# A diffusion trunk layer on one Trainium2 core: stores left under way at a stage's end, a routing search with bf16 counts, and a first gather by groups

## The reference, cut to what matters

```
def ec_moe(h, p):
    xt = h.reshape(T, D)
    aff = jax.nn.softmax((xt @ p["w_router"]).astype(F32), axis=-1)
    cap = (EC_CAPACITY_FACTOR * T) // N_EXPERTS
    vals, idx = lax.top_k(aff.T, cap)
    xs = xt[idx]
    hid = jax.nn.silu(einsum(xs, w_e_gate)) * einsum(xs, w_e_up)
    ye = einsum(hid, w_e_down) * vals[..., None]
    y = jnp.zeros((T, D)).at[idx.reshape(-1)].add(ye.reshape(-1, D))
```

## Time and profile before

| what | us |
|---|---|
| median of 3 runs | 3444.71 |
| the runs | 3438.53, 3444.91, 3444.71 |
| the profiled execution, its own time | 3445.33 |
| its span | 3443.2 |
| PE busy in it | 3199.8 (93%) |
| DVE busy | 1607.1 (47%) |
| ACT busy | 1271.0 (37%) |
| POOL busy | 363.5 (11%) |
| mean granted clock of TensorE | 0.957 |

### The profile page before, as it was taken

One profiled execution on the slowest core, in us unless ns is written; L12 is line 12 of the kernel. 1 busy time (PEld: TensorE's weight loads), 2 busy tenths in 40 slices (PEclk: granted clock), 3 DMA queues, 4 the chain that ended last, 5 costly groups with the idle time before them and its releaser, 6 DMA issues. The chain is left out here.

```text
span 3443.2 us, 51395 instructions
## 1 busy us (share of the span) xinstructions
PE 3199.8 (93%) x19321; PEld 2723.1 (79%) x19321; DVE 1607.1 (47%) x2990; ACT 1271.0 (37%) x1957; POOL 363.5 (11%) x313
## 2 busy tenths in 40 slices
PE   7899998999898799999989964999999999999996
PEld 2488886988644699989977753898888898899895
DVE  5423222533256442333235556555555555555555
ACT  4743342422243131222124531444444443344445
POOL 1111111000034100000000001111111111111122
PEclk9899999999899799999999985999999999999998
DMA  8633333321299751432125442555555555555557
GB/s 333 239 126 104 104 121 107 116 70 63 78 365 348 246 161 57 133 96 99 57 89 180 155 161 91 170 201 188 186 186 180 179 173 173 174 192 198 192 205 275
DMA packets 282677, 565.67 MB, mean 164 GB/s; under 512 B 23464, under 2 KB 162472, under 8 KB 278329
## 3 DMA queue, kind: packets, MB, share of 16 engines
q1 hardware_dynamic: 258063, 503.84, 41.9%
q0 software_dynamic: 15456, 54.88, 5.4%
q10 hardware_dynamic: 8976, 4.46, 0.5%
HBM read 434.45 MB, written 128.64 MB: 164 GB/s over the span
## 5 line engine op out<-in xcount | busy, mean ns | idle before, releaser
L71 PE MATMUL experts_bank<-experts_xT_high,experts_w_high_gu 128*128 128x272 f32 x2048 | 599.0, 292 | 6.2 <-DVE experts_w_low_gu L2998 6.2
L73 PE MATMUL experts_bank<-experts_xT_high,experts_w_low_gu 128*128 128x272 f32 x2048 | 591.4, 289 | 0.0
L72 PE MATMUL experts_bank<-experts_xT_low,experts_w_high_gu 128*128 128x272 f32 x2048 | 590.3, 288 | 0.0
L71 PEld LDWEIGHTS experts_bank<-experts_xT_high,experts_w_high_gu 128*128 128x128 f32 x2048 | 386.5, 189 | 19.1 <-issue 12.2
L72 PEld LDWEIGHTS experts_bank<-experts_xT_low,experts_w_high_gu 128*128 128x128 f32 x2048 | 386.9, 189 | 4.0
L73 PEld LDWEIGHTS experts_bank<-experts_xT_high,experts_w_low_gu 128*128 128x128 f32 x2048 | 386.9, 189 | 0.0
L2998 DVE TENSOR_TENSOR experts_w_low_gu<-experts_w_raw_gu,experts_w_high_gu 128x1024 fp32r<-128x1024 f32 x256 | 302.4, 1216 | 13.2 <-ACT experts_w_high_gu L2797 13.2
L2797 ACT ACTIVATE experts_w_high_gu<-experts_w_raw_gu 128x1024 fp32r<-128x1024 f32 x256 | 257.7, 1047 | 17.0 <-DMA experts_w_raw_gu<-in_w_stream 17.0
L71 PE MATMUL merge_pg<-merge_hT_high,merge_w_gates_high 128*128 128x436 f32 (+1 forms) x640 | 232.7, 364 | 12.5 <-DVE merge_hT_low L2093 12.5
L72 PE MATMUL merge_pg<-merge_hT_low,merge_w_gates_high 128*128 128x436 f32 (+1 forms) x640 | 231.9, 362 | 0.0
L73 PE MATMUL merge_pg<-merge_hT_high,merge_w_gates_low 128*128 128x436 f32 (+1 forms) x640 | 231.5, 362 | 0.0
(11 more groups left out here) (387 smaller groups left out, 6590.0 us busy)
## 6 DMA issues: line engine op xcount, KB each, us to landing
experts_w_raw_gu<-in_w_stream SPq DMA_DIRECT2D x256, 512.0 KB, 5.8
experts_w_raw_d<-in_w_stream SPq DMA_DIRECT2D x128, 512.0 KB, 7.5
filters_wm<-in_w_mod SPq DMA_DIRECT2D x12, 2048.0 KB, 11.6
merge_hT<-scratch_hT SPq DMA_DIRECT2D x32, 436.0 KB, 7.0
scratch_h<-out_row SPq DMA_DIRECT2D x17, 520.0 KB, 2.9
x_early<-in_xs SPq DMA_DIRECT2D x17, 512.0 KB, 5.2
scratch_hT<-tokens_hT SPq DMA_DIRECT2D x17, 512.0 KB, 4.2
scratch_qkT<-tokens_qkT SPq DMA_DIRECT2D x17, 512.0 KB, 2.8
```

The costliest lines, as they stand in the source:

```text
L71: pe.matmul(out, lhs[0], rhs[0], start=start, stop=False)
L72: pe.matmul(out, lhs[0], rhs[1], start=False, stop=False)
L73: return pe.matmul(out, lhs[1], rhs[0], start=False, stop=stop)
```

## The change

In the output stage SP no longer waits for its last stores: the four waits are kept in a list and done by SP at the head of the expert stage, which then gives POOL a semaphore (`stored`) that POOL waits for before the first gather. `x` and `row` are placed first in the stage's memory, where in the next stage only raw weights lie. `band` and `seg` are loaded in the output stage, and ACT makes a bf16 copy of `seg` at its end.

In the search, the context comparison goes from DVE to POOL (three tensor_scalar of 128x16, output bf16), the reduce is gone, and PE sums the 16 columns with 16 accumulating bf16 matmuls. The counts are bf16 (whole numbers up to 256). The context comparison with the capacity comes first, the latent one second.

The first gather has a semaphore for each group. PE turns group by group (8 blocks of one group, then the next), ACT and DVE treat a group in one instruction each; the second `index` no longer stands behind DVE's last low part.

```diff
 phase_out
+                sp.dma_start(s["band"][:], d["band"]).then_inc(s["ld_band"], 16)
+                sp.dma_start(seg[:], d["seg"]).then_inc(lds, 16)
                 stores(0, 0, 0, True)
...
                 retire(sp, s)
                 for h in range(2):
-                    sp.wait_ge(xst[h], 16 * ((NT + 1 - h) // 2) + HAD)
-                    sp.wait_ge(rst[h], 16 * ((NT + 1 - h) // 2) + HAD)
+                    s["open"].append((xst[h], 16 * ((NT + 1 - h) // 2) + HAD))
+                    s["open"].append((rst[h], 16 * ((NT + 1 - h) // 2) + HAD))
...
                 router(NT - 1, 0)
+                act.wait_ge(lds, 16)
+                act.activation(s["seg"][:], seg[:], ACT.Copy)
 phase_experts, SP
-                sp.dma_start(band[:], d["band"]).then_inc(ldb, 16)
-                sp.dma_start(seg, d["seg"]).then_inc(lds, 16)
+                for each, value in s["open"]:
+                    sp.wait_ge(each, value)
+                sp.sem_inc(stored, 1)
 PE
                 for i in range(DIGITS):
+                    pe.wait_ge(PB.sem, PB.at(i, "reach"))
+                    for t in range(CCAP):
+                        mm = pe.matmul(pn, seg_b[:, 0:P], reach[:, :, t], start=(t == 0), stop=(t == CCAP - 1))
+                    mm.then_inc(*QC.inc("sum"))
                     pe.wait_ge(RB.sem, RB.at(i, "count"))
-                    pe.matmul(pi[:, 0:6], seg[:, 0:P], cnt[:], start=True, stop=True).then_inc(*QB.inc("sum"))
+                    pe.matmul(pi[:, 0:3], seg_b[:, 0:P], cnt[:], start=True, stop=True).then_inc(*QB.inc("sum"))
...
                 index(0)
-                pe.wait_ge(ga, 48)
-                for q in range(KT):
-                    turn(q, bank[:, q, :])
-                pe.wait_ge(VX.sem, VX.at(0, f"x{KT - 1}"))
+                for n, (at, m) in enumerate(GROUPS):
+                    pe.wait_ge(g0[n], 16)
+                    for q in range(KT):
+                        mm = pe.transpose(first(n)[:, q, :], xs[0:m, n, P * q:P * q + P], s["ident"][0:m, 0:m])
+                    mm.then_inc(*P0.inc(f"g{n}"))
                 index(1)
 ACT
-                for q in range(KT):
-                    turned(0, 0, q, bank[:, q, :])
+                for n, (at, m) in enumerate(GROUPS):
+                    act.wait_ge(P0.sem, P0.at(0, f"g{n}"))
+                    act.activation(xh[:, 0, :, at:at + m], first(n), ACT.Copy).then_inc(*A0.inc(f"g{n}"))
 DVE
-                for steps in (VG, VM, VI, VX, VK, VD, VW, VF):
+                for steps in (VG, VM, VI, VX, VK, VD, VW, VF, V0):
                     steps.give(v)
+                v.sem_inc(VX.sem, KT)
...
-                    v.tensor_tensor(reach, few[:]..., cand[:, 1, :]..., ALU.is_ge).then_inc(*RB.inc("few"))
...
-                    v.wait_ge(RB.sem, RB.at(i, "few"))
-                    v.tensor_reduce(cnt[:, 3:6], reach, mybir.AxisListType.X, ALU.add).then_inc(*RB.inc("count"))
...
+                    v.wait_ge(QC.sem, QC.at(i, "sum"))
+                    v.tensor_scalar(met[:, 1, :], pn, float(CCAP), 0.0, ALU.is_ge, ALU.add,
+                                    accum_out=digit[:, 1:2]).then_inc(*RB.inc("mc"))
                     v.wait_ge(QB.sem, QB.at(i, "sum"))
...
+                for n, (at, m) in enumerate(GROUPS):
+                    v.wait_ge(A0.sem, A0.at(0, f"g{n}"))
+                    v.tensor_tensor(xl[:, 0, :, at:at + m], first(n), xh[:, 0, :, at:at + m].bitcast(F32), ALU.subtract)\
+                     .then_inc(*V0.inc(f"g{n}"))
 POOL
+                for i in range(DIGITS):
+                    if i:
+                        g.wait_ge(RB.sem, RB.at(i - 1, "cand"))
+                    else:
+                        g.wait_ge(R0.sem, R0.at(0, "bit"))
+                    for j in range(3):
+                        mm = g.tensor_scalar(reach[:, j, :], few[:], cand[:, 1, j:j + 1].bitcast(F32), None, ALU.is_ge)
+                    mm.then_inc(*PB.inc("reach"))
...
+                g.wait_ge(stored, 1)
                 gather(0, 0)
```

More of the change, by code:

```diff
@@ L2578, in phase_experts @@
         R0 = counted("dve_arrange", ["zero", "a0", "a1", "ac", "as", "prob", "few", "thr", "bit"])
-        RB = counted("dve_bits", ["few", "count", "bit", "next", "ml", "mc", "step", "cand", "thr"])
+        RB = counted("dve_bits", ["count", "bit", "next", "mc", "ml", "step", "cand", "thr"])
+        PB = counted("pool_bits", ["reach"])
         R1 = counted("dve_slots", ["gl", "gc", "need", "tl", "tc", "s0", "s1", "e0", "e1", "lim", "k0", "k1",
                                           "sel", "p0", "p1", "f0", "f1", "off", "q0", "q1", "pos", "ones"])
-        QB = counted("pe_bits", ["sum"])
+        QB, QC = counted("pe_bits", ["sum"]), counted("pe_bits_context", ["sum"])
         Q1 = counted("pe_route", ["prob", "above", "ahead", "slots", "pos"])
@@ L2586, in phase_experts @@
         PX = counted("pe_xT", [f"x{k}" for k in range(KT)])
+        P0, A0, V0 = (counted(f"{n}_xT_first", [f"g{n}" for n in range(len(GROUPS))]) for n in ("pe", "act", "dve"))
         PD = counted("pe_dn", [f"d{n}" for n in range(4)])
@@ L2986, in numbers @@
                     v.wait_ge(PI.sem, PI.at(e, "ids"))
[L2987 to L2988 removed]
+                    if e == 2:
+                        for sem in g0:
+                            v.wait_ge(sem, 16)
+                    elif e > 2:
+                        v.wait_ge(ga, e * 48 - 96)
                     v.tensor_copy(ids[:, h, 0:2], pi[:, 0:2]).then_inc(*VI.inc("i0"))
```

86 lines of the change are left out of this document (52 added, 34 removed).

## The result

The changed kernel takes **3420.01 us** (median of 4 runs, 3417.76 to 3422.66), the kernel before 3444.64 us (4 runs, 3438.53 to 3444.91): a ratio of 0.9934, 95% interval [0.9922, 0.9947].

What follows compares the result with a forecast made beforehand. A serial chain between the output stage and the gapless columns was taken as the bound; -1.0 - 1.1 + 0.2 - 9.8 - 1.3 - 4.8 = -17.8 us against 3445.33 gave 3427.5, for a median 3427, range 3421 to 3437.

Steps and rivals of the forecast that it cites:

- End of the output stage, -1.0: At the output stage's end nobody waits for the last row store any more: -1.0 us.
- two increments, +0.2: At the expert stage's start DVE has two more semaphore increments, 0.11 us each: +0.2 us.
- The band, -1.1: At the expert stage's start DVE's 1.08 us wait for the band goes, as it is loaded earlier: -1.1 us.
- The search, -9.8: In the search's 15 digits, a digit falls from 2.89 to 2.24 us, 0.65 us each: -9.8 us.
- margin of 0.1 us for POOL: In each digit POOL's three comparisons end at about 1.0 us, where about 1.1 is needed; the least certain term.
- Rival 2: In the search DVE's counts hold POOL, 0.47 us a digit slower than before: 3444, no change; chance 0.09.
- Rivals 1 and 3: Search: POOL's comparisons cost 0.4 us each, 3433, chance 0.15; each digit pays a 3.04 us hold, 3469, chance 0.05.
- The three sums, -1.3: Behind the search, three sums go from fp32 to bf16, 0.42 us less each: -1.3 us.
- The first gather, -4.8: Ahead of the columns, turning by groups hides the first group and starts columns at about 2125.9 instead of 2130.74: -4.8 us.
- PE's first turning: Sign in the profile at the first gather: PE starts turning some 6 us ahead of the last landing.

Runs made afterwards that it cites:

- e1: The kernel before, run again without an edit: 3443.78 us, ratio 1.0.
- e2: The changed kernel, run again without an edit: 3420.22 us, ratio to the kernel before 0.9934.
- e5: The kernel before with only the output stage's end changed (stores left under way, tables loaded ahead, memory laid out anew): 3439.08 us, ratio 0.9984.
- e11: The change without the first gather by groups: 3422.98 us, ratio to the kernel before 0.9935.
- e3: The kernel before with only the first gather by groups: 3439.0 us, ratio 0.9989.
- e4: The kernel before with only the new search and its bf16 sums: 3436.36 us, ratio 0.9976.
- e6: The kernel before with the new search and the gather by groups, without the output stage's changed end: 3430.87 us, ratio 0.9963.
- e10: The kernel before with DVE's comparisons for the second index held until POOL's three gather issues are out: 3437.85 us, ratio 0.9984.
- e12: The kernel before with new search and groups, plus one already met wait on POOL just ahead of the first gather: 3426.38 us, ratio 0.9949.
- e8: The change with one more POOL comparison in every digit: 3426.16 us, ratio to the kernel before 0.9951.
- e7: The change with POOL's wait for the stores moved to the start of its expert stage program: 3426.63 us, ratio to the kernel before 0.9945.
- e9: The change with DVE's comparisons for the second index held until POOL's three gather issues are out: 3424.77 us, ratio to before 0.9945.

## Why the prediction was right, and where it was off

**Right by its own steps.** The bound was read rightly: a serial chain in front of columns that then run on without a gap. From the first column to the first of the last expert's scattered adds it is 1206.0 us in e1 and 1204.6 in e2 (1204.6 to 1210.4 over the twelve), so what was gained ahead of the columns arrived at the end.

**End of the output stage, -1.0, and two increments, +0.2.** Both confirmed, the first a little larger. Router maximum to memset is 5.16 to 5.88 us in the seven profiles without the exit (mean 5.48) and 3.87 to 4.07 in the seven with it (mean 4.01): -1.5 us with what the increments cost. These belong to the groups: with the exit it is 3.87 and 3.88 us in e5 and e11, which have no groups, and 4.06 or 4.07 in the five profiles with them, so two increments cost 0.19 us, and the exit by itself is worth 1.6.

**The band, -1.1.** It is not there. Memset to band product is 2.44 us in the one profile that the forecast read, and 1.26 or 1.27 us in those of e1, e3, e4, e6, e10 and e12, which load the band as it does. The wait of 1.08 us was a late load in that execution, and a term was made of it.

**The search, -9.8.** The mechanism is right and the size slightly off: 2.33 us a digit and not 2.24. The step that failed is the margin of 0.1 us for POOL. Its start comes 0.26 us after `cand`, but the three comparisons are 0.29 us apart where 0.24 each was taken from a 128x1 row, and POOL ends at 1.16 us where 1.0 was expected and 1.1 was the latest that would do; DVE reads the context sum at 1.85 us instead of 1.75. Two of the 14 steps take 2.6 us. Over 15 digits the gain was 0.6 + 7.4 = 8.0 us.

**Rival 2, and the rule behind it, did not come.** POOL's comparisons and DVE's counts run at once with neither stretched: 0.40 us from count to count, as in the earlier trace rows. By the rule of the Trainium skill (Advanced Engine Details and Errata, VectorE Performance Modes) two-port instructions of VectorE and GpSimd's block each other; this trace shows no block for the counting form. Rivals 1 and 3 fell with the same rows.

**The three sums, -1.3.** Fifteenth `cand` to ids went from 15.82 to 14.62 us: -1.2.

**The first gather, -4.8: this is the step that was mis-sized.** It was priced with issues and landings carried over from the earlier trace rows. For the groups by themselves that held: 4.3 us (e3), 4.5 (e11 to e2). But 3.85 and 2.80 us were not the price of the issues. They were DVE's hold on them, and in the change the hold is gone: 23.7 us became 12.3 (e1 to e2), 11.4 in place of 4.8. PE's first turning came 2.8 us ahead of the last landing and not some 6. The forecast had seen a hold of 3.04 us on a small POOL operation and used it for a rival in the search, and did not ask whether the two long issues, with DVE busy beside them, were the same thing. The trace could have raised the question: of the 48 issues of this line in the kernel before the median takes 1.07 us, and the two of 128 rows here 3.85 and 2.80.

**The sum.** From e1 and e2, whose earlier stages agree within 0.12 us: exit with the increments -1.4, search -8.0, sums -1.2, gather -11.4, columns -1.4: -23.4 us. Their profiled executions differ by 3440.91 - 3417.24 = 23.7. Against these the forecast's -17.8 has 0.5 too much for exit, band and increments, 1.8 too much for the search, 0.1 too much for the sums, and 6.6 and 1.4 too little for gather and columns. The 1.4 of the columns is no larger than what they vary from profile to profile. That the total came as near as it did is in part luck: 2.4 us too much and 8.0 too little partly cancel.

**What decides whether the issues are held.** Shown: DVE's work holds them (e10, and the ends that keep their place). Why it does not in the change is open. With the first DMA 0.70 us after the ids, all six profiles beside a working DVE had long issues. With it at 1.19, behind the added wait, four had short ones (the change twice, e8, e11) and two long ones (e5, e12). That the wait must stand just ahead of the gather rests on e7. What the two long ones lack may be conditions as well: e5 the search (the groups are not one, by e11), e12 the exit's tables, its memory layout and the semaphore that is waited for. But each of these rests on one profile of one execution, and the times of e5 and e12 leave room for other executions in which the issues were short. So a hold that comes in some executions of one program and not in others is a rival that no run here settles; more profiles of e5, e7 and e12 would. In the change DVE pays a little instead: its 16 comparisons, 4.27 us in e12, are stretched to 4.75.

```profile
2092.20 4.75 DVE L3008 TENSOR_SCALAR experts_below<-experts_pos_slot 128x256 bf16<-128x256 f32 x16
```

```profile
2096.36 4.27 DVE L3004 TENSOR_SCALAR experts_below<-experts_pos_slot 128x256 bf16<-128x256 f32 x16
```

The first row is of the change, the second of e12. Most of the 0.48 us lies in three of the 16, where the others took 0.33 to 0.36 us each:

```profile
2094.03 0.48 DVE L3008 TENSOR_SCALAR experts_below<-experts_pos_slot 128x256 bf16<-128x256 f32 x1
...
2095.23 0.57 DVE L3008 TENSOR_SCALAR experts_below<-experts_pos_slot 128x256 bf16<-128x256 f32 x1
...
2096.50 0.44 DVE L3008 TENSOR_SCALAR experts_below<-experts_pos_slot 128x256 bf16<-128x256 f32 x1
```

The three issues of the change end at 2094.41, 2095.69 and 2096.84 us, each inside one of these. So near its end an issue and a comparison are in each other's way: here DVE gives way for 0.1 to 0.24 us, in e12 the issue waits 3.1 us. e11 and e12 start the DMA at the same moment against DVE's comparisons (1.19 us after the ids), and one is through in 1.17 us, the other in 4.28. What settles who gives way is not in the profile, and no run isolates it.

The Trainium skill (DMA: Bandwidth & Descriptors, SWDGE vs HWDGE vs iDMA) says that GpSimd writes the descriptors of its DMAs into SBUF, and that VectorE in a two-port mode locks it out of there. e10 agrees as to who holds whom; that the same comparisons let the issues through in the change, the page does not explain.

No version beat the change. It is the fastest run here, but 6.8 to 8.1 us of its path (e5 to e11, e7 to e2) hang on something that is not understood.

## What to carry to other kernels

Before a DMA issue's duration is carried into a sum, look at what VectorE does beside it, and compare it with the shortest issue of the same kind: here 3.85 us was a cost of 1.16. Where GpSimd's DMAs are on the path, try to let VectorE rest until they are issued: one wait gave the kernel before 7.2 us of path and 5.0 us of time. Where the issues go through anyway it costs instead: 2.0 us of path in the change (e9). A wait seen once (the band's 1.08 us) is a term only if a second execution has it, and an edit that leaves the path alone should still be read in the profile around it, since one instruction more in a stream shifts what stands behind it.

## What the runs showed of the hardware that was not expected

- A wait that is already met, put ahead of other waits in POOL's stream, delays the first indirect DMA behind it: 0.65 us of gap in place of 0.18 (e12 and e6, which differ in that wait alone).
- VectorE's plain comparisons and low parts can hold a GpSimd DMA issue, 3.85 us instead of 1.16 (e1, e10), or let it through at the price of three comparisons of 0.44 to 0.57 us instead of 0.33 (the change).
- A semaphore increment at the head of VectorE's stream costs 0.09 us (3.88 against 4.06 us for two, e5 and e11 against the change).
- GpSimd's comparison of 128x16 costs 0.29 us in a run of them, hardly more than its smallest operation here (128x1, 0.19 to 0.24 us), and holds nothing on VectorE's counts beside it.
- 16 accumulating bf16 matmuls of three columns take 0.59 us at the lower level of the clock; in e8, where DVE waits for them, it reads the sum 0.62 us after the first starts (2051.18).
- In every profile with the new search but e8's, two of the 14 steps from `cand` to `cand`, the third and the eleventh, are 0.21 to 0.29 us longer. In e2 it lies within one instruction of DVE, between a comparison and the read of its accumulator; these two rows usually start 0.08 or 0.09 us apart, here 0.31:

```profile
2050.91 0.16 DVE L2949 TENSOR_SCALAR_CACHE_REDUCE experts_met<-experts_bank 128x3 f32<-128x3 f32 x1
2051.22 0.08 DVE L2949 DVE_READ_ACCUMULATOR experts_met<-experts_bank 128x1 f32 x1 [0.15 <-issue]
```

In e8 every digit is 2.62 us. No cause was looked for.
